# Gated DeltaNet heads on one core: projection chunks of the next head between the hops of the block inverses, its key chain inside the scan, the prompt solve in a bank of its own

## What is computed

```python
qkv = jax.nn.silu(depthwise_conv(proj[..., :QKV_DIM], conv_w))   # 3 taps
q, k = l2_norm(q), l2_norm(k)
m = jnp.where(strict, einsum(kb, kc) * decay, 0.0)
tmat = lax.linalg.triangular_solve(eye + m, eye, lower=True, unit_diagonal=True)
def step(s, xs):                                                # once per chunk of tokens
    v_new = u_i - einsum(w_i, s)
    o_i = einsum(q_i * exp(g_i), s) + einsum(a_i, v_new)
    s = s * exp(g_last) + einsum(k_i * exp(g_last - g_i), v_new)
```

## Time and profile before

| what | before |
|---|---|
| median of three runs | 1910.84 us |
| the profiled execution, its own time | 1920.41 us |
| its span | 1918.6 us |
| mean granted clock of TensorE | 0.839 of full speed |
| TensorE busy | 1572.9 us (82%) |
| VectorE busy | 720.7 us (38%) |
| ScalarE busy | 501.6 us (26%) |
| GpSimd busy | 183.6 us (10%) |

### The profile page before, as it was taken

One profiled execution on the slowest core, in us unless ns is written; L12 is line 12 of the kernel. 1 busy time (PEld: TensorE's weight loads), 2 busy tenths in 40 slices (PEclk: granted clock), 3 DMA queues, 4 the chain that ended last, 5 costly groups with the idle time before them and its releaser, 6 DMA issues.

```text
span 1918.6 us, 33943 instructions
## 1 busy us (share of the span) xinstructions
PE 1572.9 (82%) x14716; PEld 1171.8 (61%) x14716; DVE 720.7 (38%) x1426; ACT 501.6 (26%) x1114; POOL 183.6 (10%) x257
## 2 busy tenths in 40 slices
PE   3998689989599895577797887978979997798992
PEld 2555467745587674556676776766765445686671
DVE  1276856424311112323534445435452625111114
ACT  2105224412111001532442432524421212110011
POOL 2100100100111111010110100101100000111120
PEclk9999679999599898576876967868769998799996
DMA  9324756223799964320101101011010435598755
GB/s 358 120 67 154 247 192 223 68 88 117 241 332 318 305 233 168 110 64 5 51 18 38 53 19 38 21 37 62 5 49 3 159 115 197 191 334 300 269 196 202
DMA packets 171540, 276.49 MB, mean 144 GB/s; under 512 B 7568, under 2 KB 111168, under 8 KB 170880
## 3 DMA queue, kind: packets, MB, share of 16 engines
q1 hardware_dynamic: 155424, 216.61, 33.9%
q0 software_dynamic: 15968, 57.71, 8.1%
HBM read 245.27 MB, written 29.02 MB: 143 GB/s over the span
## 4 chain that ended last, share of the span: by engine, by line
PE 58%; issue 20%; DVE 6%; DMA 5%; ACT 4%; POOLq 3%; POOL 1%; DVEq 1%; SPq 0%; ACTq 0%; PEldq 0%
PE psum L1749 12%; PE psum L972 6%; PE psum L1809 4%; PE psum L540 4%; POOLq L1327 3%; DMA ring<-in_w_mod 3%; PE psum L1390 2%; PE psum L310 2%; PE psum L820 2%; PE psum L2277 2%; PE psum L1761 2%; PE psum L526 1%; PE psum L799 1%; PE psum L1875 1%; DMA arena<-in_w_mod 1%
## 5 line engine op out<-in xcount | busy, mean ns | idle before, releaser
L1749 PE MATMUL psum<-hT,ring 128*128 128x384 f32 (+1 forms) x768 | 238.5, 455 | 0.4 <-ACTq L207 0.4
L1749 PEld LDWEIGHTS psum<-hT,ring 128*128 128x128 f32 x768 | 146.0, 201 | 53.1 <-issue 12.8
L1809 PE MATMUL psum<-arena 32*32 32x32 f32 x5120 | 87.2, 237 | 93.9 <-DVE arena L2192 51.9
L1390 PEld LDWEIGHTS psum<-arena,ring 128*128 128x128 f32 x1280 | 149.5, 196 | 13.0 <-issue 10.6
L1390 PE MATMUL psum<-arena,ring 128*128 128x128 f32 x1280 | 150.3, 279 | 3.8 <-DVE arena L1424 3.8
L1809 PEld LDWEIGHTS psum<-arena 32*32 32x32 f32 x5120 | 78.0, 149 | 104.2 <-issue 72.7
L1430 DVE COPY arena<-psum 128x512 f32<-128x512 f32 x36 | 24.9, 691 | 282.3 <-DMA y2d<-arena,small 239.0
L672 DVE SCALAR_TENSOR_TENSOR arena<-arena,params_sb 128x655 f32<-128x655 f32 x120 | 106.0, 911 | 4.8
L1430 ACT COPY arena<-psum 128x512 f32<-128x512 f32 x36 | 21.1, 586 | 289.4 <-DMA y2d<-arena,small 254.4
L1401 PE MATMUL psum<-ring,arena 128*128 128x512 f32 x160 | 80.8, 652 | 15.5 <-DVE arena L1454 15.5
L1401 PE MATMUL psum<-modN,arena 128*128 128x512 f32 x128 | 66.9, 672 | 15.5 <-DVE arena L1454 15.5
(11 more groups left out here) (419 smaller groups left out, 2683.2 us busy)
## 6 DMA issues: line engine op xcount, KB each, us to landing
ring<-in_w_mod SPq DMA_DIRECT2D x24, 1024.0 KB, 5.3
ring<-in_m_w_gate SPq DMA_DIRECT2D x20, 1024.0 KB, 5.6
ring<-in_m_w_up SPq DMA_DIRECT2D x20, 1024.0 KB, 9.6
ring<-in_m_w_down SPq DMA_DIRECT2D x20, 1024.0 KB, 8.0
arena<-in_w_mod SPq DMA_DIRECT2D x16, 1024.0 KB, 5.3
modN<-in_m_w_down SPq DMA_DIRECT2D x16, 1024.0 KB, 9.4
ring<-in_c_w_in SPq DMA_DIRECT2D x24, 512.0 KB, 6.2
arena<-y2d SPq DMA_DIRECT2D x20, 512.0 KB, 6.8
```

Of the source, the lines that this page charges most:

```text
L1390: m = pe.matmul(bank((2, 4)[half] + (1, 3)[half] * q, P, f * P), gu_slot[s][:, c0:c0 + P], xgT[:, q, k, :], start=(k == 0), stop=(k == KC ...
L1749: m = pe.matmul(bank(un % 2, w), ring[:, s, c0k:c0k + P], hT[:, k, o:o + w], start=(k == 0), stop=(k == KC - 1))
L1809: m = pe.matmul(bank(b, 32, 32 * i)[QD(q), :], lhs(5 * g + i, q), rhs(5 * g + i, q), start=True, stop=True)
```

## The change

Of the 48 chunks of the next head (40 of z in the last) 15 go between the hops and joins of the levels and one ahead of the prompt solve; the other 32 are spread over the scan anew. The query products and sums move to the second hop and wait apart. In the scan the next head's key chain comes earlier on all engines, its diagonal copies and first inverses are done before the scan ends, its distances and decays at the start of the head before. The prompt solve writes to banks 5 and 7 and `keys_on_state(h, 1)` follows it at once. VectorE drains and transposes group by group. Head 0's key chain is interleaved with its own projection. The amount of arithmetic is the same. The core of the diff (calls that only moved are shown at their new place):

```diff
@@ heads_pe
+        solved = lambda c, si: bank(xb(c), P, P) if si > 0 else bank(yb_(c), P, 2 * P)
             def query_products(n):
                 count_wait(pe, "hd_nt", n + 1)
                 count_wait(pe, "hd_silu", 3 * n + 2)
-                count_wait(pe, "hd_sq", n + 1)
                 for t in range(NT):
                     pe.matmul(tile_bank(t), knT[...], qf[...], start=True, stop=True)
+            def query_sums(n):
+                count_wait(pe, "hd_sq", n + 1)
                 for t in range(NT):
                     m = pe.matmul(bank(3, 1, P + t), qsq[...], C("ones")[:, 0:1], start=True, stop=True)
-            def levels(h):
+            def levels(h, fill):
...
-                    if lev == 1:
+                    if lev == 2:
                         query_products(h)
+                    else:
+                        fill(2 if lev == 1 else 1)
                     for g in range(2):
                         count_wait(pe, "hd_p", 11 * h + 2 * (lev - 1) + g + 1)
                         blocks(g, 6 + g, ...).then_inc(S("hd_tp"), 1)
+                    if lev == 2:
+                        query_sums(h)
+                        fill(1)
+                    else:
+                        fill(2)
...
+                fill(1)      # after the first paired group (L1831)
...
                 v_to_tokens(h)
+                fill(1)
...
+                fill(2)      # between the two 64x64 groups (L1850, L1860)
...
-            project(0, 0, 48)
+            project(0, 0, 24)
             k_to_tokens(0)
+            project(0, 24, 32)
             kn_to_features(0)
+            project(0, 32, 40)
             key_products(0)
+            project(0, 40, 48)
             for h in range(H):
...
+                chunks = count()
+                def fill(m):
+                    for _ in range(m):
+                        c = next(chunks)
+                        if more: project(n, c, c + 1)
+                        else: project_z(c, c + 1)
-                levels(h)
+                levels(h, fill)
+                fill(1)
                 count_wait(pe, "hd_u", 7 * (h + 1))
...
                 solve(h, 0)
+                keys_on_state(h, 1)
+                fill(3)
                 values(h, 0)
                 solve(h, 1)
+                fill(3)
                 queries_on_state(h, 1)
                 values(h, 1)
+                fill(1)
                 if more: k_to_tokens(n)
+                fill(1)
                 keys_on_state(h, 2)
+                fill(2)
                 solve(h, 2)
+                fill(2)
                 queries_on_state(h, 2)
                 values(h, 2)
                 if more: kn_to_features(n)
+                fill(2)
                 keys_on_state(h, 3)
+                fill(2)
                 solve(h, 3)
+                fill(1)
                 if more: key_products(n)
+                fill(1)
                 queries_on_state(h, 3)
                 values(h, 3)
+                fill(3)
                 keys_on_state(h, 4)
+                fill(3)
                 solve(h, 4)
+                fill(3)
                 queries_on_state(h, 4)
                 values(h, 4)
+                fill(5)
@@ heads_act, order in the loop over h
-                diagonal_blocks(h)
+                if more: distances(n, 0, 10); decays(n)
                 silu(h, 2, vf)
+                if more: take_unit(n, 0)
                 inverse_blocks(h)
+                if more: take_unit(n, 1)
                 new_values(h, 0)
+                silu(n, 0, kf)                  | last head: take_z(0), take_z(1)
                 new_values(h, 1)
+                key_norms(n), take_unit(n, 2)   | last head: take_z(2)
                 new_values(h, 2)
+                key_features(n), take_unit(n, 3)| last head: take_z(3)
                 new_values(h, 3)
+                diagonal_blocks(n), take_unit(n, 4)
                 new_values(h, 4)
                 take_unit(n, 5), silu(n, 1, qf), query_squares(n)
@@ heads_dve
-                    dve.drain()
-                    for g in range(2):
+                        dve.drain()             # level by level: now for each of the two groups
                         dve.transpose(flat(UUc, g), flat(TTc, g)).then_inc(S("hd_t"), 1)
...
+                if more: conv(n, 0, 1, kf)
+                residuals(h, 1)
                 prompt_states(h)
                 outputs(h, 0)
-                residuals(h, 1)
                 states(h, 1)
-                if more: conv(n, 0, 1, kf)
                 residuals(h, 2)
                 outputs(h, 1)
+                if more: normal_keys(n)
                 states(h, 2)
                 residuals(h, 3)
                 outputs(h, 2)
-                if more: normal_keys(n)
+                if more: transition(n)
                 states(h, 3)
                 residuals(h, 4)
                 outputs(h, 3)
-                if more: transition(n)
+                if more: unit_inverses(n)       # L2186 to L2192, before at the head's own start
                 if more: conv(n, 1, 0, qf[n % 2])
                 outputs(h, 4)
```

More of the change, by code:

```diff
@@ L10 @@
 from contextlib import ExitStack
+from itertools import count
 import numpy as np
@@ L1874, in solve @@
                         count_wait(pe, "hd_r", 8 * h + 2 * (si - 1) + c + 1)
-                    pe.matmul(bank(xb(c), P, P), UU[:, MAT[(t, d)], :], RR[:, c, :] if si > 0 else vt[h % 2][:, 0, :],
+                    pe.matmul(solved(c, si), UU[:, MAT[(t, d)], :], RR[:, c, :] if si > 0 else vt[h % 2][:, 0, :],
                               start=True, stop=True).then_inc(S("hd_tr"), 1)
@@ L1974, in distances @@
                     count_wait(act, "hd_rows", 16 * (n + 2))
+                    if n >= 2:
+                        count_wait(act, "hd_sv", 10 * (n - 1))
                 for t in range(NT):
@@ L2034, in new_values @@
                     count_wait(act, "hd_tr", 10 * h + 2 * si + c + 1)
-                    act.mul(vn[:, c, :], bank(xb(c), P, P), beta[:, t, d, h:h + 1]).then_inc(S("hd_vn"), 1)
+                    act.mul(vn[:, c, :], solved(c, si), beta[:, t, d, h:h + 1]).then_inc(S("hd_vn"), 1)
                     if si < LAST:
-                        act.mul(vs[:, c, :], bank(xb(c), P, P), dec[:, t, d, h:h + 1]).then_inc(S("hd_vn"), 1)
+                        act.mul(vs[:, c, :], solved(c, si), dec[:, t, d, h:h + 1]).then_inc(S("hd_vn"), 1)
             distances(0, 0, 10)
             decays(0)
[L2041 to L2046, removed]
-            key_norms(0)
+            take_unit(0, 0)
+            take_unit(0, 1)
+            silu(0, 0, kf)
+            take_unit(0, 2)
+            key_norms(0)
+            take_unit(0, 3)
+            key_features(0)
+            take_unit(0, 4)
+            diagonal_blocks(0)
+            take_unit(0, 5)
+            silu(0, 1, qf[0])
             query_squares(0)
-            key_features(0)
             for h in range(H):
@@ L2052, in heads_act @@
                 more = n < H
-                diagonal_blocks(h)
+                if more:
+                    distances(n, 0, 10)
+                    decays(n)
                 silu(h, 2, vf)
+                if more:
+                    take_unit(n, 0)
                 inverse_blocks(h)
+                if more:
+                    take_unit(n, 1)
                 new_values(h, 0)
                 if more:
[L2058 to L2061, removed]
+                    silu(n, 0, kf)
+                else:
                     take_z(0)
                     take_z(1)
[L2064 to L2072, removed]
+                new_values(h, 1)
                 if more:
                     key_norms(n)
[L2075 to L2078, removed]
+                    take_unit(n, 2)
+                else:
+                    take_z(2)
+                new_values(h, 2)
                 if more:
                     key_features(n)
+                    take_unit(n, 3)
+                else:
+                    take_z(3)
+                new_values(h, 3)
+                if more:
+                    diagonal_blocks(n)
                     take_unit(n, 4)
@@ L2177, in heads_dve, with unit_inverses @@
             flat = lambda v, g: v[:, of(g), :].rearrange("p a b -> p (a b)")
[L2178 to L2185, removed]
+            def unit_inverses(h):
                 count_wait(dve, "hd_own", 5 * h + 1)
@@ L2192, in heads_dve @@
                     dve.transpose(flat(TTc, g), flat(UUc, g)).then_inc(S("hd_t"), 1)
+            dve.memset(eps_col, EPS).then_inc(S("hd_zero"), 1)
+            conv(0, 0, 1, kf)
+            normal_keys(0)
+            transition(0)
+            conv(0, 1, 0, qf[0])
+            unit_inverses(0)
+            for h in range(H):
+                n = h + 1
+                more = n < H
                 conv(h, 2, 2, vf, (0,))
```

50 lines of the change are left out of this document (18 added, 32 removed).

## The result

The changed kernel took 1785.68 us in the median of four runs (1781.12 to 1795.25), the kernel before 1909.92 us beside it: a ratio of 0.9367, 95% interval 0.9316 to 0.9418. That is 124 us less, where the forecast was 73 less: inside the range of 1776 to 1894, but outside the 1800 to 1868 of the likeliest case and inside the 1765 to 1795 of the rival with the clock high almost throughout. The profiled execution took 1786.65 us, its span is 1784.8 us.

The account below looks back on a forecast made before the run. TensorE's queue was taken to set the pace, at a mean granted clock of 0.74 to 0.77. Seven heads at 8 us, 9 for head 0 and 8 for the last gave 73 us less: 1838 us, range 1776 to 1894.

Parts of the forecast that it names:

- the likeliest case: In the levels of each head the clock is up for part of the time: 8 us less per head, 1838 us, chance 0.55.
- the rival with the clock high almost throughout: Clock stays high in the levels too: 16 us less for each of seven heads, 1775 us in all, chance 0.17.

## What to carry to other kernels

Small matmuls that alone leave the clock low need wide ones among them, not behind them: the same chunks in a block behind the small ones cost 7 us a head more than between them. Moving work off a scan pays only if the other engines' orders are moved with it. When TensorE stalls on "issue" in rows of short instructions, look at the trace's instruction queue and at which large transfer runs beside it, and move that transfer: closing a gap may have moved it there; and keep GpSimd's SBUF work out of the stretch where VectorE is on the path.

## What the hardware did that I had not expected

Eighty records of 32x32 on the four diagonal tiles take 1.22 us at 1.2 GHz and 0.84 us at 2.4 GHz, 10.5 ns a record at the high clock. Beside a load of 365 to 408 GB/s TensorE stopped for 3.6 us although no operand of it was awaited; all 170 such waits end 1.19 to 1.61 us after a 16 KB packet of the instruction queue has landed. After 6.68 us of idleness and 1.29 us of small tiles, one run of four 128x384 records (2.61 us) was enough in the head shown for the next one to run at 2.4 GHz; the slowest of the seven heads had its clock back after 6.2 us.
